# First tile of the projections shared by sample and prompt rows, page row numbers earlier, one gate product earlier

## The reference, cut to what matters

```python
h = rmsnorm(x, attn_norm)
q_sb, k_sb, v_sb, z_sb, q_dl, k_dl, v_dl, z_dl = split(h @ w_in, 8)   # w_in is 1024 x 4096
# mixer A: stick-breaking attention, for the sample rows over 8192 cached tokens in pages of 128
# mixer B: q and k normed by head and rotated, then dilated windows of 128, 512 and 2048 tokens
y = concat(rmsnorm(o_sb) * silu(z_sb), rmsnorm(o_dl) * silu(z_dl))
x = x + y @ w_out
out = x + sigmoid(x @ w_ple_gate) * (p @ w_ple)
```

## Time and profile before

| | |
|---|---|
| median of 3 runs | 3076.78 us (3069.73 to 3077.31) |
| the profiled execution | 3099.58 us, its span 3097.9 us |
| mean granted TensorE clock | 0.959 |
| PE busy | 2808.1 us, 91% of the span |
| DVE, ACT, POOL busy | 1572.5, 1344.4, 749.7 us |
| mean rate of the transfers | 185 GB/s |

### The profile page before, as it was taken

How to read it: one execution, slowest core, us unless ns; L and a number is a source line. 1 busy time by engine, 2 the same in 40 slices (tenths; PEclk the granted TensorE clock), 3 DMA queues, 4 the chain that set the end, 5 groups by cost and what they waited for, 6 DMA issues and landing times. The chain is left out here.

```text
span 3097.9 us, 47359 instructions
## 1 busy us (share of the span) xinstructions
PE 2808.1 (91%) x17542; PEld 1978.9 (64%) x17542; DVE 1572.5 (51%) x2730; ACT 1344.4 (43%) x2482; POOL 749.7 (24%) x952
## 2 busy tenths in 40 slices
PE   7999989999899999998999758888888774899998
PEld 5888858888655555554888645555555442688887
DVE  3000032222588888887777633444434335666663
ACT  3212131111487777786677523333333323333332
POOL 0000001111122222223577733333333100000000
PEclk9999999999899999999999969999999987899999
DMA  6565766556300000103333389999999695323321
GB/s 209 200 215 197 235 209 210 183 203 217 112 15 28 15 28 1 42 8 100 97 84 84 80 339 407 416 419 417 408 414 407 252 374 217 126 100 108 108 87 43
DMA packets 209768, 574.16 MB, mean 185 GB/s; under 512 B 40096, under 2 KB 109184, under 8 KB 173728
## 3 DMA queue, kind: packets, MB, share of 16 engines
q0 software_dynamic: 45568, 348.22, 28.9%
q1 hardware_dynamic: 164000, 223.27, 21.9%
HBM read 494.67 MB, written 143.73 MB: 206 GB/s over the span
## 5 line engine op out<-in xcount | busy, mean ns | idle before, releaser
L495 PE MATMUL proj_ps_G<-proj_w_hi,proj_xT_hi 128*128 128x512 f32 x1024 | 399.8, 390 | 1.6 <-DVE proj_xT_lo L352 1.6
L499 PE MATMUL proj_ps_G<-proj_w_hi,proj_xT_lo 128*128 128x512 f32 x1024 | 398.6, 389 | 0.0
L497 PE MATMUL proj_ps_G<-proj_w_lo,proj_xT_hi 128*128 128x512 f32 x1024 | 398.5, 389 | 0.0
L1632 DVE COPY sbs_kT<-sbs_ps_T 128x512 f32<-128x512 f32 x256 | 173.7, 687 | 360.1 <-PE sbs_ps_T L1793 351.1
L434 ACT ACTIVATE proj_out<-proj_ps_G,proj_stat 128x512 f32<-128x512 f32 (+1 forms) x136 | 93.4, 688 | 579.5 <-PE proj_ps_G L499 574.8
L1793 PE MATMUL sbs_ps_T<-held,sbs_k_ring 128*128 128x128 f32 x2048 | 284.0, 297 | 26.8 <-ACT sbs_kT L1714 17.8
L1793 PEld LDWEIGHTS sbs_ps_T<-held,sbs_k_ring 128*128 128x128 f32 x2048 | 254.0, 155 | 64.2 <-issue 33.5
L695 POOL CAST sbp_sp_hi<-sbp_sp 128x512 fp32r<-128x512 f32 (+3 forms) x320 | 171.9, 551 | 455.8 <-DVE sbp_sp L742 455.6
L742 DVE SCALAR_TENSOR_TENSOR sbp_sp<-sbp_Z,sbp_el 128x512 f32<-128x512 f32 (+3 forms) x320 | 180.7, 606 | 88.9 <-ACT sbp_el L824 88.5
L495 PEld LDWEIGHTS proj_ps_G<-proj_w_hi,proj_xT_hi 128*128 128x128 f32 x1024 | 192.3, 188 | 41.4 <-DVE proj_xT_lo L352 1.8
L499 PEld LDWEIGHTS proj_ps_G<-proj_w_hi,proj_xT_lo 128*128 128x128 f32 x1024 | 192.2, 188 | 39.9
(11 more groups left out here) (305 smaller groups left out, 5694.0 us busy)
## 6 DMA issues: line engine op xcount, KB each, us to landing
out_k_win_s<-in_cache_k_win POOLq DMA_DIRECT2D x16, 2044.0 KB
out_v_win_s<-in_cache_v_win POOLq DMA_DIRECT2D x16, 2044.0 KB
dls_k_in<-in_cache_k_win SPq DMA_DIRECT2D x16, 1024.0 KB, 10.7
dls_v_in<-in_cache_v_win SPq DMA_DIRECT2D x16, 1024.0 KB, 14.6
proj_out<-in_w_in SPq DMA_DIRECT2D x28, 512.0 KB, 5.0
merge_o<-scratch_o_dil SPq DMA_DIRECT2D x48, 256.0 KB, 4.8
proj_x_in<-in_x_prompt SPq DMA_DIRECT2D x16, 512.0 KB, 4.4
scratch_xT_hi<-proj_xT_hi SPq DMA_DIRECT2D x16, 512.0 KB, 4.8
```

What stands on the lines that cost most here:

```text
L495: nc.tensor.matmul(ps_G[0:n, g, :], xT_hi[:, slot, k, 0:n], w_hi[:, k, cols], start=(k == 0), stop=False)
L497: nc.tensor.matmul(ps_G[0:n, g, :], xT_hi[:, slot, k, 0:n], w_lo[:, k, cols], start=False, stop=False)
L499: mm = nc.tensor.matmul(ps_G[0:n, g, :], xT_lo[:, slot, k, 0:n], w_hi[:, k, cols], start=False, stop=(k == KC - 1))
L1632: nc.vector.tensor_copy(kT[:, j, i, :], ps_T[:, x % TB, :]).then_inc(kT_odd, 1)
```

## The change

In `project` the item loop still has 17 items, but PE works items 0 and 1 in one loop over the chunks. The sample rows are multiplied as four-byte numbers (`xs`, the sum of `xT_hi` and `xT_lo`): 32 columns of the array for each of the four groups of weights, all of them into one bank `ps_S`, group `g` on partitions `32 g` to `32 g + 31`. So x of the samples and its scale are loaded four times, and the results lie on four ranges of partitions. The x of item 1 is loaded ahead of the weights. The load for item 2 stays where it was, at the head of SP's item 1.

The row numbers of the pages are made in `dilated_prompt`, on DVE ahead of its group 20, with their two loads on SP behind the first loads of that stage. In `merge`, `gate_ple(0)` stands ahead of `turn_y(2)`.

```diff
             if mixer_b:
-                load_kept(0, 0)
+                xT_parts = kept(0, 0)
+                for here, there in xT_parts[0:2]:
+                    sp.dma_start(here, there).then_inc(xs_loaded, 16)
+                for g in range(COPIES):
+                    sp.dma_start(stat[copy_of(g), 0, 2:3], xT_parts[2][1]).then_inc(xs_loaded, 16)
+                load_kept(1, 1)
             else:
-                sp.dma_start(x_in[0:NS, 0, :], x_s).then_inc(x_loaded[0], 16)
+                for g in range(COPIES):
+                    sp.dma_start(x_in[copy_of(g), 0, :], x_s).then_inc(xs_loaded, 16)
+                sp.dma_start(x_in[:, 1, :], x_p[0:P, :]).then_inc(x_loaded[1], 16)
...
-                if not last(item) and mixer_b:
-                    if not first(item):
-                        hold(sp, grp_done, GROUPS * item)
-                        hold(sp, evacuated, GROUPS * item)
+                if not last(item) and not first(item) and mixer_b:
+                    hold(sp, grp_done, GROUPS * item)
+                    hold(sp, evacuated, GROUPS * item)
                     load_kept(item + 1, 1 - slot)
...
+            def whole_sample():
+                nc.vector.tensor_tensor(xs[:, :, :], xT_hi[:, 0, :, 0:NS].bitcast(F32), xT_lo[:, 0, :, 0:NS].bitcast(F32),
+                                        ALU.add).then_inc(xs_done, 1)
...
             split(0)
             split(1)
-            if not mixer_b:
+            if mixer_b:
+                x_wait(dve, 0, 0, 0)
+                whole_sample()
+            else:
                 low_parts(0, 0, 0)
+                dve.wait_ge(lo_done, 2)
+                whole_sample()
+                low_parts(1, 1, 0)
...
             high_w(0)
             high_w(1)
             if not mixer_b:
                 high_parts(0, 0, 0)
+                high_parts(1, 1, 0)
...
+            def first_two():
+                pe.wait_ge(xs_done, 1)
+                if mixer_b:
+                    x_wait(pe, 1, 1, 0, PARTS)
+                else:
+                    pe.wait_ge(lo_done, 4)
+                for k in range(KC):
+                    pe.wait_ge(w_split, 2 * k + 2)
+                    for part in (w_hi, w_lo):
+                        for g in range(GROUPS):
+                            mm = nc.tensor.matmul(ps_S[copy_of(g), :], xs[:, k, :],
+                                                  part[:, k, g * W:(g + 1) * W].bitcast(F32),
+                                                  start=(k == 0 and part is w_hi), stop=(k == KC - 1 and part is w_lo))
...
+                    for g in range(GROUPS):
+                        cols = slice(g * W, (g + 1) * W)
+                        nc.tensor.matmul(ps_G[:, g, :], xT_hi[:, 1, k, :], w_hi[:, k, cols], start=(k == 0), stop=False)
+                        nc.tensor.matmul(ps_G[:, g, :], xT_hi[:, 1, k, :], w_lo[:, k, cols], start=False, stop=False)
+                        mm = nc.tensor.matmul(ps_G[:, g, :], xT_lo[:, 1, k, :], w_hi[:, k, cols],
+                                              start=False, stop=(k == KC - 1))
```

In `norm_rotate` and its power on POOL the samples' q and k now lie below each other (64 partitions x 512) and no longer beside each other (32 x 1024). In `dilated_prompt`, `stick_breaking_sample` and `merge`:

```diff
             load_dilated_qk(sp, t, qk_odd, 1, qk_odd_loaded)
+            sp.dma_start(every_table[:, :], t["page_table"].rearrange("b n -> (b n)").rearrange("(a n) -> a n", a=1)
+                         .to_broadcast([P, DEC_B * PAGES])).then_inc(lanes_loaded, 16)
+            sp.dma_start(lane[:, :], t["lane"][:, :]).then_inc(lanes_loaded, 16)
...
             for g in range(-2, G + 2):
+                if g == 20:
+                    page_rows()
...
-            pool.wait_ge(rows_step, 2)
+            pool.wait_ge(rows_ready, 1)
...
                     project_out(i, 1)
+                if i == 1:
+                    gate_ple(0)
                 if i + 1 < N:
                     turn_y(i + 1)
-                if i >= 1:
+                if i > 1:
                     gate_ple(i - 1)
```

More of the change, by code:

```diff
@@ L180, in project, with copy_of, x_wait @@
         stage = out[:, :, :].rearrange("p a (b d) -> p (a b) d", d=D)
+        COPIES = P // NS
         def rows_of(item):
             return NS if first(item) else P
+        def copy_of(g):
+            return slice(g * NS, (g + 1) * NS)
+        def x_wait(eng, item, slot, use, parts=1):
+            if first(item):
+                eng.wait_ge(xs_loaded, 16 * (2 + COPIES if mixer_b else COPIES))
+            else:
+                eng.wait_ge(x_loaded[slot], 16 * parts * use + (16 * parts if slot else 0))
         w_rows = t["w_in"][0].rearrange("(c p) e -> p c e", p=P)
@@ L259, in body @@
                                 .then_inc(ahead_loaded[c], 16)
-                if not last(item) and mixer_b:
-                    if not first(item):
-                        hold(sp, grp_done, GROUPS * item)
-                        hold(sp, evacuated, GROUPS * item)
+                if not last(item) and not first(item) and mixer_b:
+                    hold(sp, grp_done, GROUPS * item)
+                    hold(sp, evacuated, GROUPS * item)
                     load_kept(item + 1, 1 - slot)
[L265 to L268, removed]
+                if not last(item) and not first(item) and not mixer_b:
+                    hold(sp, x_squared, item)
+                    hold(sp, x_turned, 2 * item)
                     load(item + 1, 1 - slot)
@@ L281, in body @@
                     dst = dst_s[g] if first(item) else dst_p[g][bass.ts(item - 1, P), :]
-                    sp.dma_start(dst, out[0:n, slot, g * W:(g + 1) * W]).then_inc(stored[g][slot], 16)
+                    made = out[copy_of(g), 0, 0:W] if first(item) else out[:, slot, g * W:(g + 1) * W]
+                    sp.dma_start(dst, made).then_inc(stored[g][slot], 16)
             steps(sp, body)
@@ L440, in body @@
                                 act.wait_ge(ssum_done, item)
-                            nc.scalar.activation(qk_sq[0:n, :], out[0:n, slot, 0:2 * W], ACT.Square) \
+                            done = (slice(0, 2 * NS), slice(0, W)) if first(item) else (slice(0, P), slice(0, 2 * W))
+                            nc.scalar.activation(qk_sq[done[0], done[1]], out[done[0], slot, done[1]], ACT.Square) \
                                 .then_inc(sq_done, 1)
-                        elif not last(item):
+                        elif not last(item) and not first(item):
                             high_parts(*following(item, slot, use))
@@ L487, in body @@
+            def body(item, slot, use):
+                if first(item):
+                    first_two()
+                    return
+                if isinstance(item, int) and item == 1:
                     if not mixer_b:
@@ L489, in body @@
                     return
+                if mixer_b:
+                    x_wait(pe, item, slot, use, PARTS)
+                else:
+                    pe.wait_ge(lo_done, 2 * item + 2)
+                n = P
                 for g in range(GROUPS):
-                    if not first(item):
-                        pe.wait_ge(evacuated, GROUPS * item - GROUPS + g + 1)
+                    pe.wait_ge(evacuated, GROUPS * item - GROUPS + g + 1)
                     for k in range(KC):
@@ L1449, in _, with stick_breaking_sample @@
                         turn_in(p + 1, f, OB[:, :])
[L1452 removed]
+def stick_breaking_sample(nc, t, held, rows, paged_loaded, rows_ready):
     C = H * DEC_S
@@ L2646, in build @@
         paged_loaded = nc.alloc_semaphore(name="paged_loaded")
-        with nc.sbuf_tensor("held", [P, 2 * TILES * P], F32) as held:
+        rows_ready = nc.alloc_semaphore(name="rows_ready")
+        with nc.sbuf_tensor("held", [P, 2 * TILES * P], F32) as held, \
+                nc.sbuf_tensor("rows", [P, DEC_B * GROUPS_OF_PAGES], I32) as rows:
             project(nc, t, 0, held, ahead_loaded, pair_loaded)
```

124 lines of the change are left out of this document (62 added, 62 removed).

## The result

The changed kernel takes 3109.22 us (median of 4 runs, 3106.54 to 3112.12), the kernel before 3075.02 in the same comparison: a ratio of 1.0113, 95% interval 1.0101 to 1.0125. It is 34 us slower; 3080 was forecast, and the range ended at 3093.

What follows compares the result with a forecast made beforehand. PE was to bound the load phase and the dilated part, transfers the paged part. Terms -1.3 + 11.5 - 5.0 + 0.2 - 2.2 = +3.2 us gave 3102.8 profiled, 3080 as median; range 3066 to 3093.

Steps and rivals of the forecast that it cites:

- The price of the four-byte products: Shared loop on PE: four run beside each other for the price of one, so 8 cost 1.79 us a chunk.
- By the row it is nothing, and I take nothing: Shared loop on PE: the 16 changes between 32-column and 128-column products in a half cost nothing.
- a drain: Tiling-mode changes in PE's shared loop: if each cost a product's overlap, 0.16 us x 16 = 2.6 us a half.
- DVE gets 1.4 us of work where it has 9 us in 50 free. I take 0.2: Dilated part: the row numbers' DVE work is covered by PE, which bounds that part; 0.2 us lost.
- without it it would cost 1.4: Dilated part: without PE as cover, the row numbers' work on DVE would cost 1.4 us.
- 11.5 us lost: Projections, second half: item 2's loads follow item 1's stores, so it starts 8.9 us late and cold, 2.6 more.
- 4.4 us of landing: Second half, pause ahead of item 2: the loads for item 2 land 4.4 us after their issue.
- 1.3 us gained: Projections, first half: item 2 starts at 63.8 and loses 2.6 cold, so 66.4 against 67.65.
- all of the 12 us: First half: item 1 ends at 55.7, 12 us before the old 67.65, but item 2's load waits for item 0's stores.
- The rows for the page numbers (5.0): Paged part: with row numbers made earlier, the paged block and first gather begin 5.0 us earlier; 5.0 us gained.
- the gate (2.2): `merge`: `gate_ple(0)` fits PE's idle 10.8 us ahead of `turn_y(2)`, and `turn_p(1)` comes earlier; 2.2 us gained.
- The slow rival: Second half, rotation to item 2: window-buffer copy holds SP and loads longer; 3089, or 3093 with later starts; chance 0.24.

Runs made afterwards that it cites:

- The runs at groups 20, 25 and 40: Only the page row numbers moved, ahead of that group of the dilated part, against the kernel before: 3085.06, 3068.72 and (one run) 3084.60 us.
- the one with sums: Only the row numbers moved, ahead of group 20, their four casts written as sums, against the kernel before: 3079.21 us in one run.
- the run with early loads only: Projections' change alone, SP's loads for item 2 ahead of item 0's stores in both halves, against the kernel before: 3080.47 us, ratio 1.0018.

## Why the prediction was wrong, point by point

- **The price of the four-byte products was right, that of the changes between 32 and 128 columns was not.** Eight four-byte products cost 1.86 us in a chunk (1.79 forecast). "By the row it is nothing, and I take nothing" rested on one distance of the earlier trace rows, from a last 32-column round to the next start; the distances ahead of and behind the changes come to 0.3 us in a chunk. A chunk took 4.84 us and not 4.51, and the loop 40.8 and 40.4 us in the two halves, not 38.6. The 2.4 us of a half are near the 2.6 that the prediction had worked out for a drain and then left out; whether they are a drain no run shows.
- **The largest failure is "DVE gets 1.4 us of work where it has 9 us in 50 free. I take 0.2".** It cost 14.6. The bound, "without it it would cost 1.4", rested on the duration that these instructions have beside an idle POOL. The runs at groups 20, 25 and 40 and the one with sums show that a cast or a product with constants from SBUF to SBUF stands still until POOL's casts are over, here up to 13.5 us. DVE's free share says nothing on that. I read DVE's and PE's rows of this stretch and not POOL's, which has four casts of 3.9 us where the prediction put the new work. The Trainium skill's "GPSIMD Engine Reference", section "Specifications", says that POOL's SBUF interfaces are shared with VectorE and contend with DVE instructions in a two-port mode or with two SBUF inputs. The Trainium skill's "VectorE: DVE Perf Modes", section "Mode 2×_2P — use both read ports for one tensor", says that this mode is for one source in SBUF, for copies and for operations with constants. The trace agrees for the cast and the product (13.5 and 11.96 us). The sum (0.38 us), which that section does not name, did not wait, and neither did a reciprocal of 8 columns from SBUF (0.19 us).
- **"11.5 us lost" in the second half was the right mechanism at half its size**: 22.5. Of the 11 us missing, PE's start is 2.4 (431.90 less 419.58, against 422.8 less 412.9), the loop 1.8, and the pause ahead of item 2 is 6.3 longer. In that pause the chain through the norms took 8.2 us (7.8 reckoned) and SP's hold 4.9 (4.7), but from the first load's issue to PE's start it took 11.4 us and not 5.3. The term at fault is "4.4 us of landing": the last load landed after 10.5 us. The prediction placed the copy of item 1, and rightly ("just as long before": 8.1 us ahead of the loads, 8.7 before); it left out POOL's next copy. That one follows the norms of item 1, which now end right behind those of item 0, and so it slid from 3.5 us behind the first load to 0.5 ahead of it. The fourteen profiles have 944 loads of x or its parts. The 13 of them that were issued up to 2 us behind a copy of POOL's landed after 10.0 to 18.6 us; the other 931, all at least 8.7 us behind one or with none ahead, have a median of 4.3 and a longest of 10.7. No run moved the next copy alone.
- **"1.3 us gained" in the first half** was +7.0 to +7.4 (419.6 and 420.0 against 412.6), or +5.2 to +5.6 against the mean of 414.4. Item 2 began at 66.48, where the prediction had its first product at 63.8. That 66.48 looks like its 66.4 is chance, since the 66.4 has the slow start in it, which in the trace comes on top (1.7 us for 2.6 reckoned). The 2.7 us are 0.6 of a later start and 2.2 of a longer loop. So already up to item 2 it was 0.6 us lost. The rest of the 6.7 us between this profile and the first one before lies behind it, where the sum had no term: 3.2 us for the pause ahead of item 3, whose load falls into the stores of items 0 and 1 and 1.9 us behind a window copy (65.40), 1.6 for the slow start after that pause, and 1.3 for a longer pause near the end of the half. That the load for item 2 costs all of the 12 us is shown by the run with early loads only in part: the pause moves to item 3.
- **The rows for the page numbers (5.0) and the gate (2.2)** were nearly right: 4.6 and 1.4 by the means of all profiles with and without each edit (5.4 and 1.9 in the table), and the pause of 7.12 us ahead of `turn_p(1)` stands where I put it.
- **The base.** I took the difference between the profiled execution and the median (23 us) as even; it lay in the paged part alone (690.0 against 664.9). That cost the forecast nothing, but it hides 25 us of the loss in a plain comparison of the first two profiles.
- The slow rival had its place right, between rotation and item 2, and its price from the longest landing, 8.9 us, too small; the last load landed after 10.5 us there, and after 14.8 in the first half.
- **The sum.** The forecast was +3.2 us, and the two profiles differ by 36.0. The dilated part accounts for 14.4 of the 32.8 us between them, the second half for 11.0 and the first for 8.3.

## What to carry to other kernels

When an item's work is slid under a loading phase, ask what was slid under *that item*: its results, and with them the loads queued behind their stores, come at the end of the longer phase, and nothing covers them. Ask the same of other queues: POOL's copies slid too, and one of them to just ahead of the loads. A queue that serves both stores and loads in item order turned 21.8 us that were to be saved into a pause, and a load ahead of the stores moves the pause one item on. Before DVE work is put into a stage because DVE has time, look at what POOL does at that very point.

## What the runs showed of the hardware

- A DVE cast of 32 x 128 elements, 0.2 to 0.4 us where POOL does not cast, took 13.5 us beside POOL's four casts of 128 x 2048, which follow each other, and ended with the last of them; three kernels show it, at groups 20 and 40. Sums from SBUF (0.38 us each) and copies from PSUM (0.68 us) did not wait.
- A load from DRAM landed after 4.3 and 4.6 us when SP issued it just ahead of POOL's 2 MB copy, and its neighbours after 10.3 to 12.7 us when they were issued up to 0.8 us behind it (two kernels, one profile each). All 13 loads of x issued up to 2 us behind such a copy took 10.0 to 18.6 us, and the median of the others is 4.3.
- In the loop that changes between products on 32 and on 128 columns, the distances around the changes are 0.10, 0.11 and 0.09 us longer than elsewhere.
- A profiled execution can be 25 us slow in one transfer-bound stage (406 and not 413 GB/s over 653 us of it) with every other stage within 1.1 us of the next profile. Compare stage by stage, with two profiles of the base.
